# Neighbourhood mix of a two-layer hybrid encoder: values as the weights, transposed probabilities of two query tiles as the moving side

## The reference, cut to what matters

```
h = rms_norm(x, g);  z = h @ w_in           # q, k, v of both kinds, and the gate
# neighbourhood attention, for each head; a query sees 8 grid rows x 16 columns
s = q . k * 64**-0.5 + bias(relative row, relative column)     # masked outside
p = softmax(s);  o = p @ v
x = x + (concat[diff_attention, neighbourhood] * silu(gate)) @ w_out
```

## Time and profile before

| | us |
|---|---|
| median of 3 runs | 1595.33 (1591.39 to 1595.7) |
| the profiled execution, own time | 1600.08 |
| its span, first to last instruction | 1598.3 |
| PE busy | 1528.3 (96%) |
| PEld busy | 1265.0 (79%) |
| DVE, ACT, POOL busy | 900.4, 706.3, 489.8 |
| granted TensorE clock, mean | 0.975 of full |

### The profile page before, as it was taken

How to read it: one execution, slowest core, us unless ns; L and a number is a source line. 1 busy time by engine, 2 the same in 40 slices (tenths; PEclk the granted TensorE clock), 3 DMA queues, 4 the chain that set the end, 5 groups by cost and what they waited for, 6 DMA issues and landing times. The chain is left out here.

```text
span 1598.3 us, 25900 instructions
## 1 busy us (share of the span) xinstructions
PE 1528.3 (96%) x8800; PEld 1265.0 (79%) x8800; DVE 900.4 (56%) x1948; ACT 706.3 (44%) x1402; POOL 489.8 (31%) x434
## 2 busy tenths in 40 slices
PE   7899999999999999889999999999999999998995
PEld 6688878887888888778787888788878888877874
DVE  6567676766445555552436767677654555555322
ACT  5345554545344444432424555555544434344330
POOL 2333333334313132101643242424342223220161
PEclk9999999999999999789999999999999999997997
DMA  6401010020202020301110110001211110121012
GB/s 196 94 27 40 26 39 26 29 61 21 70 21 69 20 68 20 125 1 53 53 40 27 34 33 33 33 33 33 57 34 51 40 49 30 59 81 51 27 53 105
DMA packets 38964, 78.50 MB, mean 49 GB/s; under 512 B 18801, under 2 KB 18801, under 8 KB 38897
## 3 DMA queue, kind: packets, MB, share of 16 engines
q1 hardware_dynamic: 38896, 77.62, 15.3%
HBM read 66.07 MB, written 15.47 MB: 51 GB/s over the span
## 5 line engine op out<-in xcount | busy, mean ns | idle before, releaser
L805 PE MATMUL proj<-h_hi,w_hi 128*128 128x512 f32 x1184 | 505.3, 427 | 27.0 <-DVE h_lo L1101 10.5
L807 PE MATMUL proj<-h_hi,w_lo 128*128 128x512 f32 x1184 | 470.0, 397 | 0.0
L806 PE MATMUL proj<-h_lo,w_hi 128*128 128x512 f32 x1184 | 467.3, 395 | 0.0
L500 POOL TENSOR_TENSOR w_lo<-w_raw,w_hi 128x1024 fp32r<-128x1024 f32 x78 | 188.4, 2415 | 388.5 <-ACT w_hi L634 388.5
L805 PEld LDWEIGHTS proj<-h_hi,w_hi 128*128 128x128 f32 x1184 | 225.2, 190 | 101.5 <-issue 55.4
L807 PEld LDWEIGHTS proj<-h_hi,w_lo 128*128 128x128 f32 x1184 | 224.8, 190 | 52.1
L806 PEld LDWEIGHTS proj<-h_lo,w_hi 128*128 128x128 f32 x1184 | 226.3, 191 | 34.8
L1198 DVE TENSOR_TENSOR pt_lo<-turn,pt_hi 128x512 fp32r<-128x512 f32 x192 | 132.1, 688 | 155.3 <-ACT pt_hi L676 155.2
L676 ACT ACTIVATE pt_hi<-turn 128x512 fp32r<-128x512 f32 x192 | 115.0, 599 | 230.0 <-PE turn L898 230.0
L1190 DVE CUSTOM_DVE_ANT_0 prob<-scores,dist 128x1024 f32<-128x1024 f32 x128 | 156.0, 1219 | 38.5 <-PE scores L841 36.8
L700 ACT ACTIVATE prob<-prob,nm,escale_now 128x1024 f32<-128x1024 f32 x128 | 158.2, 1236 | 0.4 <-DVE nm L1194 0.4
(11 more groups left out here) (156 smaller groups left out, 2508.0 us busy)
## 6 DMA issues: line engine op xcount, KB each, us to landing
w_raw<-chunks SPq DMA_DIRECT2D x81, 512.0 KB, 3.5
mixed_dram<-gate SPq DMA_DIRECT2D x28, 256.0 KB, 2.1
edge<-bias_dram SPq DMA_DIRECT2D x32, 224.0 KB, 3.8
h_lo<-mixed_dram SPq DMA_DIRECT2D x14, 512.0 KB, 6.6
xt<-x_t SPq DMA_DIRECT2D x8, 512.0 KB, 9.5
out_t<-prob SPq DMA_DIRECT2D x8, 512.0 KB, 3.0
bias_dram<-bias_rows SPq DMA_DIRECT2D x16, 240.0 KB, 5.7
v_next<-chunks SPq DMA_DIRECT2D x1, 512.0 KB, 6.8
```

The costliest lines, as they stand in the source:

```text
L500: pool.tensor_tensor(w_lo[:, b], w_raw[:], f32(w_hi[:, b]), ALU.subtract).then_inc(w_lo_done, 1)
L805: pe.matmul(dst, a_hi, b_hi, start=start, stop=False)
L806: pe.matmul(dst, a_hi, b_lo, start=False, stop=False)
L807: return pe.matmul(dst, a_lo, b_hi, start=False, stop=stop)
```

## The change

The mix of an NA group works on pairs of tiles. The values are the weights, and the transposed probabilities of the two tiles, side by side in `pt_hi` and `pt_lo`, are the moving side of 256 columns. `v_hl` holds [hi0 lo0 lo1 hi1], so one weight load brings the hi and lo columns of a head, and each block of keys takes two matmuls of 256 columns per head. The two tiles of an inner pair see six blocks between them: four common to both, and one at each end that only one tile uses, of 128 columns. An edge pair is so 16 matmuls and an inner pair 24 (16 of 256 columns and 8 of 128); `weigh_pair` runs in even steps only.

The result is [2 x 64 rows (hi, lo) x 256 queries] per head. ACT copies the one half of the rows and DVE adds the other (64 rows x 256 each, two instructions each), and DVE multiplies by the gate. No output is transposed. In its place the reciprocal sums, spread by POOL over 64 columns per head (`widen`, one per tile), are transposed (`turn_r`, two per pair) and multiplied into the gate ahead of time (`scaled`).

The fifth block of an inner tile is transposed in full width (128 columns of `prob`, of which 64 are zeros written once a layer), and its parts are written over 128 rows. For room, `prob` shrinks from four rows of 1024 to three (a DA group's second map has one buffer in place of two, with a wait of DVE for its own `combine` before), the distance table `dist` shares its place with `inner` and is stored to DRAM at the start and loaded back before the second layer, and `px_hi` and `px_lo` go.

```diff
-            if t >= 2:
+            if na and t % 2 == 0:
+                use(("R", t // 2 - 1), False)
+            if not na and t >= 2:
                 use(("U", t - 2), False)
...
-        prob = sb("prob", [P, 2, 2, S])
-        pt_hi = sb("pt_hi", [P, 2, HALF], F32R)
-        pt_lo = sb("pt_lo", [P, 2, HALF], F32R)
-        px_hi = sb("px_hi", [HD, 256], F32R)
-        px_lo = sb("px_lo", [HD, 256], F32R)
-        dist = sb("dist", [P, OFF + S], FP16)
+        prob = sb("prob", [P, 3, S])
+        pt_hi = sb("pt_hi", [P, 2, SPAN], F32R)      # SPAN = 5 * 2 * P
+        pt_lo = sb("pt_lo", [P, 2, SPAN], F32R)
...
+                sp.dma_start(dist_dram, dist).then_inc(dist_out, 16)
...
+                    reached(sp, scores_read, 2 * Group(l, True, NA_G - 1).step(NT))
+                    sp.wait_ge(dist_out, 16)
+                    sp.dma_start(dist, dist_dram).then_inc(dist_in, 16)
...
+            def widen(g, t, before=None):                            # POOL
+                pool.wait_ge(rrec_done, g.step(t) + 1)
+                if t % 2 == 0 and (t or before):
+                    last = g.use("R", t // 2 - 1) if t else before.use("R", PAIRS - 1)
+                    pool.wait_ge(turned, last + 1)
+                begin(pool, "pool")
+                pool.tensor_copy(rrec_wide[:, t % 2].rearrange("p (m e) -> p m e", e=HD),
+                                 rrec[:, t % 4, :].unsqueeze(2).to_broadcast([P, 2, HD])).then_inc(wide_done, 1)
...
+                    if front and front.na:          # after w_lo_part, silu, normalise; before q_lo_part
+                        widen(front, ft, g if g.na else None)
...
             def p_part(g, t, c):
-                reached(act, pv_done, g.step(t))
+                reached(act, pv_done, g.mixed(t))
...
             def output_half(g, t):                                   # ACT
...
                 if g.na:
-                    for m in range(2):
-                        last = act.activation(u_hi[:, m * HD:(m + 1) * HD], mix[:, m * P:m * P + HD], ACT.Copy,
-                                              scale=rrec[:, b, m:m + 1])
+                    act.wait_ge(pair_done, g.pairs(t // 2))
+                    act.activation(u_pair[0:HD], mix[HD:P, 0:2 * P], ACT.Copy)
+                    act.activation(u_pair[HD:P], mix[0:HD, 2 * P:4 * P], ACT.Copy).then_inc(u_half, 1)
...
-                    output_half(g, t - 1)
+                    if not g.na or t % 2 == 0:
+                        output_half(g, t - 1)
...
+            def weigh_pair(g, t):                                    # PE
+                k0 = KEY0[t - 1] // 2
+                both = slice(0, 2 * P)
+                parts = [(k, k, both, slice(k * 2 * P, (k + 1) * 2 * P)) for k in range(4)]
+                if INNER[t]:
+                    parts = [(k, k, both, slice(k * 2 * P, (k + 1) * 2 * P)) for k in range(1, 5)]
+                    parts += [(0, 0, slice(0, P), slice(0, P)), (5, 0, slice(P, 2 * P), slice(P, 2 * P))]
+                for m in range(2):
+                    for n, (k, _, to, at) in enumerate(parts):
+                        out = mix[:, m * 2 * P + to.start:m * 2 * P + to.stop]
+                        weights = v_hl[:, k0 + k, m * P:(m + 1) * P]
+                        pe.matmul(out, weights, pt_hi[:, m, at], start=n == 0, stop=False)
+                        last = pe.matmul(out, weights, pt_lo[:, m, at], start=False, stop=n == len(parts) - 1)
+                return last
+
+            def turn_r(g, t):                                        # PE
+                dst = turn_wait(g, "R", t // 2)
+                pe.wait_ge(wide_done, g.tiles(t) + 1)
+                for a in range(2):
+                    last = pe.transpose(dst[:, a * P:(a + 1) * P], rrec_wide[:, a], ident[:])
+                last.then_inc(turned, 1)
...
                     fill(2)
-                    if t >= 2:
-                        turn_u(g, t - 2)
-                    weigh(g, t - 1)
+                    if not g.na:
+                        if t >= 2:
+                            turn_u(g, t - 2)
+                        weigh(g, t - 1)
+                    elif t % 2 == 0:
+                        turn_r(g, t - 1)
+                        weigh(g, t - 1)
...
-                    if t == NT:
+                    if t == NT and not g.na:
                         turn_u(g, NT - 1)
...
+            def scaled(g, t):                                        # DVE
+                src, cols = turn_bank(True, ("R", t // 2))[:, 0:2 * P], pair_cols(True, t)
+                dve.wait_ge(turned, g.use("R", t // 2) + 1)
+                dve.wait_ge(gate_silu, 2 * g.group() + TILE[True][t] // 4 + 1)
+                dve.tensor_tensor(gate[:, cols], src, gate[:, cols], ALU.mult).then_inc(turn_freed, 1)
+
+            def output_pair(g, t):                                   # DVE
+                n, cols = g.mixed(t), pair_cols(True, t)
+                dve.wait_ge(u_half, n + 1)
+                dve.tensor_tensor(u_pair[0:HD], mix[0:HD, 0:2 * P], u_pair[0:HD], ALU.add)
+                dve.tensor_tensor(u_pair[HD:P], mix[HD:P, 2 * P:4 * P], u_pair[HD:P], ALU.add).then_inc(u_done, 1)
+                reached(dve, u_done, n + 1)
+                reached(dve, turn_freed, g.use("R", t // 2) + 1)
+                dve.tensor_tensor(gate[:, cols], u_pair, gate[:, cols], ALU.mult).then_inc(pair_done, 1)
```

More of the change, by code:

```diff
@@ L134, in kind_step, with mixed, pairs, tiles @@
             return self.l * (DA_G * NT) + self.i * NT + t
+        def mixed(self, t):
+            if self.na:
+                return self.l * MIXES + DA_G * NT + self.i * PAIRS + t // 2
+            return self.l * MIXES + self.kind_step(t) - self.l * DA_G * NT
+        def pairs(self, p):
+            return (self.l * NA_G + self.i) * PAIRS + p
+        def tiles(self, t):
+            return (self.l * NA_G + self.i) * NT + t
         def group(self):
@@ L233, in hybrid_encoder, with prob_of, pair_cols, pair_part @@
         lam_e = sb("lam_e", [P, 2, DEPTH])
-        squares = prob[:, 0, 0, :]
-        square = prob[:, 0, 1, :]
-        square_b = prob[:, 1, 0, :]
+        dist = inner[:].rearrange("p h k -> p (h k)").bitcast(FP16)[:, 0:OFF + S]
+        squares, square, square_b = (prob[:, i, :] for i in range(3))
+        flat = prob[:].rearrange("p m s -> p (m s)")
+        dist_table = flat[:, S:S + OFF + S].bitcast(I32)
         second_raw = v_next[:].rearrange("p (t c) -> p t c", c=P)
-        wq_hi = pt_hi[:].rearrange("p h (t c) -> p (h t) c", c=P)
-        wq_lo = pt_lo[:].rearrange("p h (t c) -> p (h t) c", c=P)
+        wq_hi, wq_lo = (b[:].rearrange("p h c -> p (h c)")[:, 0:S].rearrange("p (t c) -> p t c", c=P)
+                        for b in (pt_hi, pt_lo))
         lam_in = gate[:, 0:4 * DEPTH * HD].rearrange("p (a l d) -> p a l d", a=4, l=DEPTH)
-        normed = [prob[:, 1, 0, :], prob[:, 1, 1, :], square, squares]
+        normed = [square_b, gate[:], square, squares]
+        u_pair = u[:].rearrange("p b c -> p (b c)")
+        NA_AT = {(0, 0): 0, (1, 0): S, (1, 1): S + 640, (0, 1): S + 1280}
+        def prob_of(na, t, m, first, end):
+            if na:
+                at = NA_AT[t % 2, m]
+                return flat[:, at + first:at + end]
+            return prob[:, 2 if m else t % 2, first:end]
+        def pair_cols(na, t):
+            return slice(TILE[na][t - t % 2] * P, (TILE[na][t - t % 2] + 2) * P)
+        def pair_part(buf, t, c):
+            tile_of = slice(t % 2 * P, (t % 2 + 1) * P)
+            spans = buf[:].rearrange("p m (s q) -> p m s q", q=2 * P)
+            later = t % 2 and INNER[t]
+            if c == 2:
+                return spans[:, :, 0 if later else 4, tile_of]
+            return spans[:, c, 1:5, tile_of] if later else spans[:, c, 0:4, tile_of]
         scores = ctx.enter_context(nc.psum_tensor("scores", [P, 2, S], F32))
@@ L882, in turn_v @@
                                         ident[:])
[L883 removed]
+                last.then_inc(turned, uses)
             def turn_p(g, t, c):
@@ L913, in weigh @@
                 else:
-                    for m in range(2):
-                        k0, o = KEY0[t] // 2, m * P
-                        for k in range(4):
-                            at = slice(k * P, (k + 1) * P)
-                            pe.matmul(mix[:, o:o + P], pt_hi[:, m, at], v_hl[:, k0 + k, o:o + P], start=k == 0,
-                                      stop=False)
-                            last = pe.matmul(mix[:, o:o + HD], pt_lo[:, m, at], v_hl[:, k0 + k, o:o + HD],
-                                             start=False, stop=k == 3 and not INNER[t])
-                        if INNER[t]:
-                            pe.matmul(mix[:, o:o + P], px_hi[:, o:o + P], v_hl[0:HD, k0 + 4, o:o + P],
-                                      start=False, stop=False)
-                            last = pe.matmul(mix[:, o:o + HD], px_lo[:, o:o + P], v_hl[0:HD, k0 + 4, o:o + HD],
```

(22 more changed lines are left out.)

128 lines of the change are left out of this document (68 added, 60 removed).

## The result

The changed kernel takes 1530.88 us (median of four runs, 1530.2 to 1533.38) against 1594.99 for the kernel before measured beside it: ratio 0.9604, 95% interval 0.9587 to 0.962, 64.1 us less. The forecast was 1531, 64.4 less. Its profiled execution took 1533.38 with a span of 1531.5, 66.8 under the span of before (1598.3, whose mean granted clock of 0.975 is low for this kernel: other executions of it beside the experiments had 0.975 to 0.985, mostly 0.98 and more).

The account below looks back on a forecast made before the run. PE's own stream was taken to bound six of eight NA groups: 6 x (7.4 + 1.0) = 50.4 us, plus 14 for the two last groups, 64.4 off 1595.3, forecast 1531 (chance 0.73), range 1518 to 1545.

Parts of the forecast that it names:

- Price of a 256-column matmul: In the NA mix, a 256-column matmul bringing its own weights costs 0.119 us, between 0.112 and 0.17.
- Rivals A: In the mix, the 256-column matmul is dearer, 0.17 us, so the kernel takes 1558 us; chance 0.09.
- B: In the mix, load and stream don't overlap, 0.23 us a matmul at the dearest, time 1587 us; chance 0.04.
- Edge pair: Mix of two edge tiles: 3.60 us falls to 1.90, two transposes before and after cancel, 1.70 saved.
- Inner pair: Mix of two inner tiles: 5.26 us falls to 3.24 with transposes and the full-width fifth block, 2.0 saved.
- the group's 7.4: Saving in an NA group without its border: two edge pairs at 1.70 and two inner pairs at 2.0 us.
- Border: Between two NA groups, the output transpose and its wait go: 1.0 us saved at each of six borders.
- the prediction's lower case: At a border only 0.4 us is saved, if the next tile's transpose then waits for the split of the values.
- Two last groups: Last NA group of each layer, partly at half clock: 7 us saved each, 14 together, from 2 to 12 each.
- The stall on POOL's spread: In the last groups, tile 1's spread stands behind the SiLU, so the first pair's mix can't start before about 659.
- rival D: Each pair's mix waits for POOL's spread: 2.5 us a pair is 80 us, time 1611, slower; chance 0.04.
- rival C: In NA groups, output in one piece delays DVE 0.8 us on 32 pairs: 26 us given back, 1557; chance 0.10.

Follow-up runs that it names:

- e1: Changed kernel with each 256-column matmul of the pair mix made as two of 128 columns, so more loads, same columns: 1587.73 us.
- e3: Changed kernel where, for the first head of each pair, matmuls with lo probabilities load only the 64 hi columns of the values: 1527.31 us.
- e7: Changed kernel with DVE splitting the next values ahead of the last gate product at borders of two NA groups: 1528.63 us.
- e2: Changed kernel with the pair mix's 256-column matmuls covering only the first tile's 128 columns, same number of loads: 1528.0 us.
- e8: Changed kernel with an extra POOL instruction of about 1.7 us in front of every spread of reciprocals: 1533.1 us.
- e6: Changed kernel with DVE's copy of the inner tiles' bias one step later in every NA group: 1531.03 us.
- the control: The changed kernel as it is, run once more beside three of the follow-up experiments on the same chip: 1531.38 us.

## Why the prediction was right, point by point

*Price of a 256-column matmul:* 0.119 forecast, 0.120 measured. It was read as the rest of a pair of unlike matmuls in the earlier trace rows, and e1 to e3 show why that held: the pace is one weight load of 0.112 as long as the stream is shorter than that, and 256 columns are just about as long. The changed kernel has half the loads on the edge tiles and 24 for 40 on the inner ones. Rivals A and B are out, and with B the estimate of 0.21 from the Trainium skill's rule on row groups (TensorE: Matmul & The Clock Gate, The mechanism): a stream of 256 columns and a load of 128 on the same rows start every 0.120.

*Edge pair:* saved 1.70 forecast. Measured at a steady pair 2 x 1.91 before (one transposed output in each) and 2.22 after, 1.6; the first pair of a group had one output transpose only, 1.5. The mis-sized term is "two transposes for two cancel". *Inner pair:* 3.06 measured with its transposes, against 2.80 + 0.29 = 3.09.

*Step without a mix:* a cost that I had left out. PE goes from the projection (last start 483.70) straight to scores (484.02), 0.32 where the next projection would come after 0.23. Four such steps are 0.3 to 0.4 us a group. With this and the edge pairs the group's 7.4 becomes about 6.9, and 7.0 was measured without a border at like clock.

*Border:* 1.0 forecast. Measured in layer 1 as the difference of a group with a border and one without, 7.95 - 7.0 = 0.9; in layer 2 0.7 to 0.9. Half of the prediction's lower case came true inside it: the next transpose does wait for the values, 0.3 to 0.8. So the sign "no wait over 0.4" failed in layer 2. e7 gives that wait back.

*Two last groups:* the term that was too small, 14 for 22.6, which is 13.6 in layer 1, above the term's own upper end of 12, and 9 in layer 2. The windows of the first one show a part of it. Before, two stretches ran below full clock (span, busy times, clock in the eighth column); after, one:

```profile
660.00:684.00 24.00, 21.05 (x84) 17.37 (x85) 13.48 (x29) 9.72 (x18) 2.37 (x1) 0.58 0.25 97
...
700.00:710.00 10.00, 8.66 (x31) 7.01 (x32) 5.46 (x11) 2.51 (x6) 0.00 (x0) 0.66 0.00 1
```

```profile
637.00:652.00 15.00, 10.68 (x50) 8.33 (x50) 10.32 (x19) 7.43 (x13) 2.98 (x3) 0.66 0.51 196
```

The second last group, before and after:

```profile
1440.00:1460.00 20.00, 17.70 (x70) 14.42 (x70) 13.51 (x28) 9.72 (x18) 2.36 (x1) 0.54 0.19 70
```

```profile
1380.00:1400.00 20.00, 14.14 (x75) 11.12 (x74) 15.14 (x28) 10.91 (x19) 2.68 (x2) 0.86 0.34 132
1400.00:1420.00 20.00, 17.49 (x97) 13.98 (x97) 13.41 (x30) 9.66 (x19) 0.59 (x2) 0.91 0.00 1
```

A clock of 0.58 is 84% of the stretch at 1.2 GHz. In layer 1 that is 20 us and 7 us at half speed before and 10 us after; at half speed a busy microsecond does half the work, so with PE's busy share of each stretch about 8 us of the gain are clock. In layer 2 it is 18 us before and 6 and 4 us after, which gives about 5. The mixes that ran cold before are partly gone, and the odd step's wait for its output with them. I had named both: the lower end of 2 left the clock's part out, the upper end of 12 had it in, and the 7 that I took is less than the full-clock saving of 7.4 by itself, so it left nothing for the clock. No experiment takes the clock away alone, so this split is an estimate from two executions, and the clock scatters: over the first 60 us of layer 1's last stretch it was 0.80 before and in e1, 0.91 and 0.94 in the two executions of the changed kernel, but 0.83 in e2, whose matmuls are the shortest. Why it fell less after the change stays open.

The gain comes late in these groups. From the transposes of the values to the first matmul on a loaded row it was 24.3 us before and 24.0 after in layer 1, 23.9 and 24.7 in layer 2. What the shorter mix saved up to there, PE spent waiting for POOL's spread and for the row. That waiting was not in the sum.

*The stall on POOL's spread* was named for the first pair of the last groups ("can't start before about 659"), and is 2.9 us in both. e8 shows the rest of POOL's term: 105 us more of it cost at most a few, so rival D is out as a loss in every pair; its sign, a wait of `turn_r` for POOL, appeared twice. *DVE's output in one piece* (rival C): in full groups PE waited only at the borders. The output instructions are 0.42 to 0.43 each on DVE, as priced, and 0.38 on ACT.

*What I had at nothing and wasn't:* what stands beside POOL's weight split. The copy of the bias took 0.75 before and 2.9 in both last groups after. But before, it was the split of the loaded row, right behind the copy, that stood in that place:

```profile
664.34 0.75 DVE L1260 COPY inner<-edge 128x1152 f32<-128x1152 f32 x1
...
665.91 2.48 DVE L1268 TENSOR_TENSOR h_lo<-h_lo,h_hi 128x1024 fp32r<-128x1024 f32 x1 [0.32 <-ACT h_hi L722]
```

So the two together took 0.75 + 2.48 = 3.2 us before and 2.90 + 1.23 = 4.1 after, and the change cost 0.9 in a last group by this, not 2.1. e6, which puts the row's split back into that place, shows the same: the cost belongs to the place, not to the copy.

In sum the mechanism was right: full groups limited by PE, and a mix paid by its weight loads. That the number came out within 0.3 us is luck, for two errors cancelled. The full groups with their borders came out 4.4 us under, the last ones 8.6 over. The rest is scatter: 1.9 us lost in stretches whose work didn't change, and 2.7 by which the profiled pair lies further apart (66.8) than the medians (64.1).

## What to carry to other kernels

Where PE is busy and its matmuls are narrower than the 256 columns at which load and stream were balanced here, count the weight loads, not the columns: read the distance between starts, and swap the roles of the operands so that the side with fewer different blocks is the weights. A pair of unlike matmuls in the trace gives the price of the shape that isn't there yet. When a step gets shorter, look at what now stands beside what on DVE and POOL, and at the one place where a helper engine's order was never tight before.

## What the runs showed of the hardware

A copy on DVE from SBUF to SBUF of 128 x 1152 took 0.75 us alone and 2.90 with a POOL subtraction (2.39 us) that had started 0.1 us earlier; a subtraction on DVE with both inputs in SBUF 1.23 alone and 2.57 in the same place. The two POOL instructions, in the control and in e6:

```profile
637.74 2.39 POOL L557 TENSOR_TENSOR w_lo<-w_raw,w_hi 128x1024 fp32r<-128x1024 f32 x1 [3.42 <-ACT w_hi L704]
```

```profile
641.96 2.39 POOL L557 TENSOR_TENSOR w_lo<-w_raw,w_hi 128x1024 fp32r<-128x1024 f32 x1 [4.76 <-ACT w_hi L704]
```

They end at 640.13 and 644.35. With its own length alone behind that, the copy would end at 640.88 and the split at 645.58; they ended at 640.74 and 645.43. So both end about as if they had stood still until POOL was done. The Trainium skill (SBUF — State Buffer, Who interferes with whom) says that a DVE copy in a mode that takes both of its ports contends with GpSimd for a shared pair, which whoever issues first holds for the whole instruction while the other is blocked, and that a DVE instruction with two SBUF inputs contends in the same way with a GpSimd instruction that reads SBUF; this case's rows agree. Exchanging which of the two stands there won nothing (e6, 1531.03 against 1531.38).

In steady runs at the full clock a matmul with its own 128-column load started every 0.112 us, with 64 and 128 columns in turn (before) and with 128 alone (e1), every 0.120 at 256 and every 0.230 at 512; with every second load of 64 columns it was 0.115 at 256.
